# Second projection: the cast of the weight tiles moved from GpSimd to ScalarE

## The chip, the cores and the metric

The kernel runs on one core of a Trainium2 chip. The metric is the device time of one execution in microseconds (us), lower is better. All data is float32.

## The reference

Two transformer-like layers stand one behind the other, over 2048 latent tokens and 256 context tokens of width 1024. The part that matters here is the entry of the second layer: the tokens are normalised and projected by one 1024 x 2816 weight, and the first 1024 output channels feed a gated depthwise convolution of 31 taps over the tokens.

```python
def dwconv(x, w, b):            # w: 31 taps x 512 channels
    y = lax.conv_general_dilated(x, w[:, None, :], (1,), [(K // 2, K // 2)], ...)
    return y + b

def conformer_conv(a_val, a_gate, conv_w, conv_b, ln_g, ln_b):
    u = a_val * sigmoid(a_gate)
    u = dwconv(u, conv_w, conv_b)
    ...                         # layer norm, silu
```

The other 1792 channels are queries, keys, values and gates for attention and the output projection.

## The kernel before, in words

`program` (line 2892) runs the stages one after the other, each in its own scope that ends with a barrier of all engines. The stage of this document is `norm_project` (line 162), called for the second layer as `p2` with `conv` given (line 2929). The same function serves the other two layers without `conv`; the lines that differ are chosen by `if conv`.

The first half of the function normalises the tokens and leaves them transposed in SBUF as `hT`, split in a high part (fp32r) and a low part (the rest), 8 slices of 128 channels by 2304 tokens. The second half, from line 419, multiplies by the weight. It is cut in M = 22 tiles of 128 output channels. A tile `n` is a 128 x 1024 piece of weight, double-buffered (`w_sb[n % 2]`), and it is also split: `split_high` (line 144) casts it to fp32r, `split_low` (line 149) subtracts that from the original. Each product is three matmuls (high x high, high x low, low x high, lines 157 to 159).

The engines run own queues, in this order:

- SyncE (lines 442 to 459) loads the weight of tile `n` once the split of tile `n-2` is done. At tiles 4, 6, 8, 9, 11, 13 and 14 it also stores the finished convolution group `i-2` (`keep_taps`) and loads the inputs of the next one (`load_group`), which were written by the projection itself. `load_group(i)` waits for the stores of the projection tiles that it reads, for the taps of group `i-2` and for the gating of group `i-1`.
- GpSimd (lines 463 to 471) makes cast and low part of each tile `n` from 1 on. It waits for the load, and until TensorE has finished tile `n-2`, whose buffer it is.
- TensorE (lines 475 to 483) waits for the split of tile `n` and then does its chunks of tokens: four of 512 and one of 256, 24 matmuls each, every chunk in its own PSUM bank.
- ScalarE (lines 540 to 550) copies each chunk out of PSUM, with a sigmoid for the gate tiles, and issues the store of the chunk before it. `k` counts the chunks, `n, c = divmod(k, 5)`.
- VectorE (lines 495 to 527) does the convolution alone: eight groups, each of 128 channels by half of the tokens. Even groups have 2 runs of 512 tokens, odd ones a third of 256 for the context. A group is gated (line 508), gets its first tap by a tensor_scalar for each run (line 517) and the other 30 taps by one scalar_tensor_tensor for each run and tap, both inputs in SBUF (line 520); each waits for the tap before it on the same run. Line 508 is a tensor_tensor.

The first eight tiles are ordered so that gate and value of the same channels are neighbours, so that the convolution can start when two tiles are stored. Weight tile 0 is split already in the first half of the function (line 326).

`w_high` counts the casts and `w_split` the low parts.

Of the kernel before, what the change touches and what calls it, by code (L numbers as in the profile page):

```python
# [143 lines left out]
def split_high(eng, high, x):  # L144

    return eng.tensor_copy(high, x)  # L146


def split_low(eng, low, x, high):

    return eng.tensor_tensor(low, x, high.bitcast(F32), ALU.subtract)  # L151
# [10 lines left out]
def norm_project(nc, name, x_lat, x_ctx, mod, gain, w, out, groups, ident, eps, later=(), conv=None):  # L162
# [9 lines left out]
    with ExitStack() as ctx:  # L172
# [7 lines left out]
        def weight_tiles():  # L180
            tiles = [s.sb(f"w{u}", [P, KT, P]) for u in range(2)]
            parts = [[s.sb(f"w{u}_{part}", [P, KT, P], F32R) for part in ("high", "low")] for u in range(2)]
            return tiles, parts, s.sems("w_full", 2), s.sem("w_high"), s.sem("w_split")

        weights = None if later else weight_tiles()
        with ExitStack() as ctx1:
# [31 lines left out]
            with nc.Block() as block:  # L218
                @block.sync
                def _(sp):  # L220
                    def load_x(t):
                        src, n, _, _ = TILES[t]
                        if t >= NX:
                            sp.wait_ge(xn_full, t - NX + 1)
                        sp.dma_start(x[t % NX][:], src[n * P:(n + 1) * P, :]).then_inc(x_full[t % NX], 16)
# [22 lines left out]
                    for l, (c, c_ctx, _, _, _) in enumerate(later):  # L248
                        sp.dma_start(cond[:, l, 0, :], c[0].rearrange("(p k) -> p k", k=KT)).then_inc(cond_in, 16)
                        sp.dma_start(cond[:, l, 1, :], c_ctx.rearrange("(p k) -> p k", k=KT)).then_inc(cond_in, 16)  # L250
# [133 lines left out]
        w_sb, w_part, w_full, w_high, w_split = weights or weight_tiles()  # L384
# [5 lines left out]
        b_full, b_free = s.sems("b_full", 5), s.sems("b_free", 5)  # L390
        M = len(COLS)
        CTX_BEFORE = [sum(with_ctx for _, with_ctx in COLS[:n]) for n in range(M + 1)]

        def chunks(n):
            return list(enumerate(CHUNKS if COLS[n][1] else CHUNKS[:-1]))

        def uses(n, c):

            return CTX_BEFORE[n] if c == 4 else n
# [19 lines left out]
        with nc.Block() as block:  # L419
# [41 lines left out]
            @block.gpsimd  # L461
            def _(pool):
                for n in range(0 if later else 1, M):
                    pool.wait_ge(w_full[n % 2], (n // 2 + 1) * 16)
                    if n >= 2:
                        c = 4 if COLS[n - 2][1] else 3
                        pool.wait_ge(b_full[c], uses(n - 1, c))
                    pool.sem_inc(w_part_turn, 1)
                    split_high(nc.gpsimd, w_part[n % 2][0][:], w_sb[n % 2][:]).then_inc(w_high, 1)
                    pool.wait_ge(w_high, n + 1)  # L470
                    split_low(nc.gpsimd, w_part[n % 2][1][:], w_sb[n % 2][:], w_part[n % 2][0][:]).then_inc(w_split, 1)

# [12 lines left out]
            def copy_out(eng, copy, n, mine):  # L485
                if n >= 2:
                    eng.wait_ge(o_out[n % 2], n // 2 * 16)
                for c, (t0, cnt) in chunks(n):
                    if c in mine:
                        eng.wait_ge(b_full[c], uses(n, c) + 1)  # L490
                        copy(o[n % 2][:, t0:t0 + cnt], ps[c][:, 0:cnt]).then_inc(b_free[c], 1)  # L491
# [40 lines left out]
            @block.scalar  # L532
            def _(act):
                def store_chunk(k):
                    n, c = divmod(k, 5)
                    t0, cnt = CHUNKS[c]
                    act.wait_ge(b_free[c], n + 1)
                    act.dma_start(out[COLS[n][0] * P:(COLS[n][0] + 1) * P, t0:t0 + cnt], o[k % NO][:, 0:cnt]).then_inc(o_out[k % NO], 16)

                for k in range(5 * M if conv else 0):  # L540
                    n, c = divmod(k, 5)
                    cnt = CHUNKS[c][1]
                    if k >= NO:
                        act.wait_ge(o_out[k % NO], 16 * (k // NO))
                    act.wait_ge(b_full[c], n + 1)
                    nc.scalar.activation(o[k % NO][:, 0:cnt], ps[c][:, 0:cnt], ACT.Sigmoid if n < 8 and n % 2 == 0 else ACT.Copy).then_inc(b_free[c], 1)
                    if k:
                        store_chunk(k - 1)
                if conv:
                    store_chunk(5 * M - 1)  # L550
                for n in range(0 if conv else M):
                    copy_out(act, nc.scalar.copy, n, (1, 3))
                    for c, _ in chunks(n):
                        act.wait_ge(b_free[c], uses(n, c) + 1)
                    m, width = COLS[n][0], T if COLS[n][1] else SEQ
                    act.dma_start(out[m * P:(m + 1) * P, 0:width], o[n % 2][:, 0:width]).then_inc(o_out[n % 2], 16)
                for u in range(NO):
                    act.wait_ge(o_out[u], 16 * len(range(u, 5 * M if conv else M, NO)))
# [2490 lines left out]
```

## Time and profile before

| | us |
|---|---|
| median of 3 runs | 7279.33 (7265.52 to 7285.22) |
| the profiled execution | 7282.06, its span 7280.4 |
| TensorE busy, of the span | 5664.7 (78%) |
| VectorE busy | 3688.1 (51%) |
| GpSimd busy | 2075.9 (29%) |
| ScalarE busy | 1714.0 (24%) |

The profile is one execution. Times are us from the start of the span. PE is TensorE's matmuls, PEld its weight loads, DVE is VectorE, ACT ScalarE, POOL GpSimd, SP SyncE; a letter q behind an engine is its queue. A row of a timeline gives the start, the duration, the engine, the line of the source, the operation, what is written and read, and how many instructions were merged; in square brackets stands how long the engine had idled and what released it. An instruction that is held up after its start shows as a long one. Lines 146, 151 and 157 to 159 are helpers, so their rows hold several callers; the names of the tiles tell them apart (`p_w` is the weight tile, `p_cy` the convolution's sum).

### The profile page before, as it was taken

The page shows a single profiled execution, that of the slowest core. Times are in us where ns is not written, and L with a number is a line of the kernel's source. Part 1 is how long each engine was busy: PE and PEld are TensorE (multiplying, and loading weights), DVE is VectorE, ACT ScalarE, POOL GpSimd, SP SyncE. Part 2 cuts the span into 40 slices and gives each one's busy share as a digit, 9 for nine tenths or more (in the row PEclk, how much of TensorE's full clock was granted, in tenths as well). Part 3 has the DMA queues.
Part 4 walks back from the last instruction along what each step waited for, and adds up shares of the span by engine and source line. Part 5 has one row for each costly group of instructions (what it writes and reads, how often), then busy time and mean ns, then how long its engine had stood idle before and what let it go on. Part 6 is the DMA issues. An engine that isn't in the chain of part 4 may idle for free. (4 is left out here: it accounts for less than half of the span.)

```text
span 7280.4 us, 117918 instructions
## 1 busy us (share of the span) xinstructions
PE 5664.7 (78%) x49713; PEld 4331.2 (59%) x49713; DVE 3688.1 (51%) x5261; ACT 1714.0 (24%) x3014; POOL 2075.9 (29%) x1372
## 2 busy tenths in 40 slices
PE   6899971139999556749586854999986999779989
PEld 1588850028888445627475732555574887357767
DVE  2100026654444666748499235888855000256667
ACT  2100002123332322213310021444413000124442
POOL 2211100024453312203467300766734111000002
PEclk8899985569999778879698986999996999879899
DMA  6312113332111111036322122000063211121115
GB/s 206 103 66 73 68 65 119 115 101 65 56 56 47 51 45 51 10 132 206 94 95 77 65 107 72 17 18 16 15 204 105 75 66 68 62 67 26 26 57 176
DMA packets 395963, 572.21 MB, mean 79 GB/s; under 512 B 62982, under 2 KB 296070, under 8 KB 375806
## 3 DMA queue, kind: packets, MB, share of 16 engines
q1 hardware_dynamic: 351126, 394.12, 17.4%
q10 hardware_dynamic: 33576, 127.83, 4.4%
q0 software_dynamic: 10752, 42.89, 2.1%
q8 instruction: 390, 6.39, 0.4%
q14 instruction: 119, 0.97, 0.0%
HBM read 360.86 MB, written 203.90 MB: 78 GB/s over the span
## 5 line engine op out<-in xcount | busy, mean ns | idle before, releaser
L157 PE MATMUL p_bank<-p_hT_high,p_w_high 128*128 128x512 f32 (+1 forms) x2928 | 1105.3, 377 | 139.4 <-POOL p_w_low L151 121.5
L158 PE MATMUL p_bank<-p_hT_low,p_w_high 128*128 128x512 f32 (+1 forms) x2928 | 1103.7, 377 | 0.0
L159 PE MATMUL p_bank<-p_hT_high,p_w_low 128*128 128x512 f32 (+1 forms) x2928 | 1102.7, 377 | 0.0
L491 DVE COPY p_o<-p_bank 128x512 f32<-128x512 f32 (+1 forms) x142 | 90.7, 639 | 1256.5 <-PE p_bank L159 1256.5
L146 POOL CAST p_w_high<-p_w 128x1024 fp32r<-128x1024 f32 x79 | 334.4, 4233 | 1345.7 <-issue 1152.6
L157 PEld LDWEIGHTS p_bank<-p_hT_high,p_w_high 128*128 128x128 f32 x2928 | 555.9, 190 | 242.1 <-POOL p_w_low L151 122.8
L158 PEld LDWEIGHTS p_bank<-p_hT_low,p_w_high 128*128 128x128 f32 x2928 | 555.7, 190 | 99.9
L159 PEld LDWEIGHTS p_bank<-p_hT_high,p_w_low 128*128 128x128 f32 x2928 | 555.1, 190 | 100.3
L2334 POOL TENSOR_TENSOR at_acc<-at_acc,at_p 128x512 f32<-128x512 f32 x256 | 426.4, 1665 | 142.2 <-ACT at_p L2272 120.5
L2376 DVE TENSOR_REDUCE at_mx<-at_mb 128x2 f32<-128x1024 f32 (+1 forms) x292 | 356.9, 1222 | 107.7 <-PE at_mb L2175 105.9
L1197 PE MATMUL rsc_db<-rsc_W,rsc_TK 64*64 64x64 f32 x8640 | 382.6, 219 | 4.6 <-issue 3.8
L2272 ACT ACTIVATE at_p<-at_sc 128x1024 f32<-128x1024 f32 (+1 forms) x296 | 284.9, 1013 | 400.3 <-PE at_sc L2164 348.4
L520 DVE SCALAR_TENSOR_TENSOR p_cy<-p_cu,p_wt,p_cy 128x512 f32<-128x512 f32 (+1 forms) x600 | 372.5, 700 | 0.0
L491 ACT COPY p_o<-p_bank 128x512 f32<-128x512 f32 x114 | 67.0, 588 | 1281.2 <-PE p_bank L159 1281.2
L157 PE MATMUL o_bank<-o_w_high,o_m_high 128*128 128x512 f32 x800 | 314.6, 393 | 66.9 <-POOL o_m_low L151 66.9
L1197 PEld LDWEIGHTS rsc_db<-rsc_W,rsc_TK 64*64 64x64 f32 x8640 | 355.1, 136 | 5.6 <-issue 4.5
L158 PE MATMUL o_bank<-o_w_low,o_m_high 128*128 128x512 f32 x800 | 313.4, 392 | 0.0
L159 PE MATMUL o_bank<-o_w_high,o_m_low 128*128 128x512 f32 x800 | 313.2, 391 | 0.0
L1169 POOL TENSOR_TENSOR rsc_TK<-rsc_TK,rsc_lv 128x768 f32<-128x768 f32 x108 | 195.8, 1813 | 329.4 <-DVE rsc_TK L1343 329.4
L2196 PE MATMUL at_ob<-at_p,at_V 128*64 128x512 f32 (+1 forms) x1184 | 283.3, 599 | 0.7 <-ACT at_osb L2279 0.7
L1575 DVE TENSOR_TENSOR hg_P<-hg_sc,hg_mk 128x1024 f32<-128x1024 f32 x192 | 225.8, 1218 | 110.7 <-PE hg_sc L1648 110.3
L1352 DVE TENSOR_TENSOR rsc_W<-rsc_W,rsc_db 128x512 f32<-128x512 f32 x270 | 171.1, 634 | 207.5 <-PE rsc_db L1197 205.8
(375 smaller groups left out, 11285.8 us busy)
## 6 DMA issues: line engine op xcount, KB each, us to landing
rsc_X<-rwkv_chunks SPq DMA_DIRECT2D x108, 320.0 KB, 4.5
pT<-p_o ACTq DMA_DIRECT2D x28, 1152.0 KB, 4.2
pT<-p_o ACTq DMA_DIRECT2D x29, 1024.0 KB, 3.9
o_z<-pT SPq DMA_DIRECT2D x50, 512.0 KB, 5.3
o_y<-y SPq DMA_DIRECT2D x50, 512.0 KB, 6.7
pT<-p_o ACTq DMA_DIRECT2D x88, 256.0 KB, 2.0
p_w<-in_w_in_dram SPq DMA_DIRECT2D x33, 512.0 KB, 3.9
x<-o_o ACTq DMA_DIRECT2D x32, 512.0 KB
```

Of the source, the lines that this page charges most:

```text
L146: return eng.tensor_copy(high, x)
L157: nc.tensor.matmul(out, lhs[0], rhs[0], start=start, stop=False)
L158: nc.tensor.matmul(out, lhs[0], rhs[1], start=False, stop=False)
L159: return nc.tensor.matmul(out, lhs[1], rhs[0], start=False, stop=stop)
L520: x = nc.vector.scalar_tensor_tensor(dst, src, wt[:, t, k:k + 1], dst, ALU.mult, ALU.add)
L1169: nc.gpsimd.tensor_tensor(tk[:, K_LB:K_LB + LV, d, :], tk[:, K_A:K_A + 1, d, :].broadcast_to([P, LV, P]), lv[:, d, :, :], ALU.mult).then_i ...
L1197: return nc.tensor.matmul(out, l, r, start=start, stop=stop)
L1575: nc.vector.tensor_tensor(PR[n % 2][h][:], sc[h][:], mk[:, d], ALU.mult).then_inc(sc_evac[h], 1)
L2196: m = nc.tensor.matmul(ob[h * HD:(h + 1) * HD, 0:n], V[:, tiles[j], kv * HD:(kv + 1) * HD], pr[t % 4][:, h, 0:n], start=(j == 0), stop=(t ...
L2272: nc.scalar.activation(pr[t % 4][:, :, 0:n], sc[t % 2][:, :, 0:n], ACT.Exp, scale=SC).then_inc(exp_done, 1)
L2334: nc.gpsimd.tensor_tensor(acc[b % 2][:, 1, 0:n], acc[b % 2][:, 1, 0:n], pr[t % 4][:, 1, 0:n], ALU.add).then_inc(sum_b, 1)
L2376: r = nc.vector.reduce_max(mx[b % 2][:, :, t:t + nt, c], mb[:, :, 0:nt * n].rearrange("p h (j k) -> p h j k", j=nt), AX)
```

## The change

In the stage with `conv`, GpSimd no longer casts the weight tile; the low part stays there and waits for the cast as before. ScalarE makes the cast instead: for tile 1 ahead of its first copy, and for tile `n+1` between its copies of chunk 0 and chunk 1 of tile `n`. Ahead of the cast it waits for the load of the weight tile and for the end of tile `n-1` on TensorE. GpSimd keeps its own waits. The two other calls of the function, without `conv`, are as before.

```diff
--- before.py
+++ after.py
@@ -466,7 +466,8 @@
                         c = 4 if COLS[n - 2][1] else 3
                         pool.wait_ge(b_full[c], uses(n - 1, c))
                     pool.sem_inc(w_part_turn, 1)
-                    split_high(nc.gpsimd, w_part[n % 2][0][:], w_sb[n % 2][:]).then_inc(w_high, 1)
+                    if not conv:
+                        split_high(nc.gpsimd, w_part[n % 2][0][:], w_sb[n % 2][:]).then_inc(w_high, 1)
                     pool.wait_ge(w_high, n + 1)
                     split_low(nc.gpsimd, w_part[n % 2][1][:], w_sb[n % 2][:], w_part[n % 2][0][:]).then_inc(w_split, 1)
 
@@ -537,9 +538,19 @@
                     act.wait_ge(b_free[c], n + 1)
                     act.dma_start(out[COLS[n][0] * P:(COLS[n][0] + 1) * P, t0:t0 + cnt], o[k % NO][:, 0:cnt]).then_inc(o_out[k % NO], 16)
 
+                def cast_weights(n):
+                    act.wait_ge(w_full[n % 2], (n // 2 + 1) * 16)
+                    if n >= 2:
+                        act.wait_ge(b_full[4], n - 1)
+                    nc.scalar.copy(w_part[n % 2][0][:], w_sb[n % 2][:]).then_inc(w_high, 1)
+
+                if conv:
+                    cast_weights(1)
                 for k in range(5 * M if conv else 0):
                     n, c = divmod(k, 5)
                     cnt = CHUNKS[c][1]
+                    if c == 1 and 2 <= n + 1 < M:
+                        cast_weights(n + 1)
                     if k >= NO:
                         act.wait_ge(o_out[k % NO], 16 * (k // NO))
                     act.wait_ge(b_full[c], n + 1)
```

## Rows read from the trace of the kernel before

**Rows 1.** Costliest groups of the page: line, engine, operation, count | busy us, mean ns
```profile
L146 POOL CAST p_w_high<-p_w 128x1024 fp32r<-128x1024 f32 x79 | 334.4, 4233 | 1345.7 <-issue 1152.6
```

**Rows 2.** Line 546: count, ns min/median/max, first and last start in us
```profile
L546 ACT ACTIVATE p_o<-p_bank x110: 383/597/602, 3582.4 to 4234.3; 128x512 f32<-128x512 f32 x88, 128x256 f32<-128x256 f32 x22
L546 ACT ACT_TABLE_LOAD  x1: 1283/1283/1283, 3574.8 to 3574.8; - x1
```

**Rows 3.** Groups of the stage, 3540 to 4260 us
```profile
L146 POOL CAST p_w_high<-p_w 128x1024 fp32r<-128x1024 f32 x22 | 275.3, 12514 | 282.7 <-PE p_bank L159 141.2 <-issue 140.6 <-POOLq L37 0.9
...
L151 POOL TENSOR_TENSOR p_w_low<-p_w,p_w_high 128x1024 fp32r<-128x1024 f32 x22 | 58.9, 2675 | 1.8
```

**Rows 4.** Waits of the stage: us in total, times, longest
```profile
PE p_bank L157 <- POOL p_w_low L151: 103.2, 5, 28.9
```

**Rows 5.** Timeline of GpSimd in the stage: start us, us, engine line
```profile
3651.02 30.60 POOL L146 CAST p_w_high<-p_w 128x1024 fp32r<-128x1024 f32 x1 [21.15 <-issue]
...
3684.86 1.23 POOL L146 CAST p_w_high<-p_w 128x1024 fp32r<-128x1024 f32 x1
...
3796.82 50.01 POOL L146 CAST p_w_high<-p_w 128x1024 fp32r<-128x1024 f32 x1 [4.22 <-issue]
3846.90 3.21 POOL L151 TENSOR_TENSOR p_w_low<-p_w,p_w_high 128x1024 fp32r<-128x1024 f32 x1
```

**Rows 6.** Timeline of VectorE in the stage
```profile
3638.62 1.24 DVE L508 TENSOR_TENSOR p_cu<-p_cu,p_cg 128x1039 f32<-128x1039 f32 x1 [44.72 <-DMA p_cg<-pT]
...
3640.89 39.83 DVE L520 SCALAR_TENSOR_TENSOR p_cy<-p_cu,p_wt,p_cy 128x512 f32<-128x512 f32 x60
...
3689.14 51.70 DVE L520 SCALAR_TENSOR_TENSOR p_cy<-p_cu,p_wt,p_cy 128x512 f32<-128x512 f32 x90
...
3792.98 1.32 DVE L517 TENSOR_SCALAR p_cy<-p_cu,p_wt,p_cb 128x512 f32<-128x512 f32 x3
3794.22 51.71 DVE L520 SCALAR_TENSOR_TENSOR p_cy<-p_cu,p_wt,p_cy 128x512 f32<-128x512 f32 x90
```

**Rows 7.** Timeline of ScalarE in the stage
```profile
3650.96 0.39 ACT L546 ACTIVATE p_o<-p_bank 128x256 f32<-128x256 f32 x1 [2.28 <-PE p_bank L159]
...
3656.43 0.60 ACT L546 ACTIVATE p_o<-p_bank 128x512 f32<-128x512 f32 x1 [5.08 <-PE p_bank L159]
...
3675.61 0.38 ACT L546 ACTIVATE p_o<-p_bank 128x256 f32<-128x256 f32 x1 [2.27 <-PE p_bank L159]
...
3692.18 0.60 ACT L546 ACTIVATE p_o<-p_bank 128x512 f32<-128x512 f32 x1 [16.18 <-PE p_bank L159]
...
3858.37 0.60 ACT L546 ACTIVATE p_o<-p_bank 128x512 f32<-128x512 f32 x1 [36.57 <-PE p_bank L159]
```

**Rows 8.** Stretch after a stall: busy us of engines, TensorE's clock, DMA share, GB/s
```profile
3850.00:3853.00 3.00, 2.83 (x7) 2.25 (x8) 3.00 (x3) 0.00 (x0) 2.92 (x3) 0.50 0.41 110
```

**Rows 9.** Line 637, casts in the output projection: ns min/median/max
```profile
L637 ACT CAST o_w_high<-o_w x24: 1044/1046/1057, 3279.1 to 7099.3; 128x1024 fp32r<-128x1024 f32 x24
```

**Rows 10.** GpSimd and VectorE timelines in the HGRN stage; line 1468's durations
```profile
2403.97 3.46 POOL L1468 TENSOR_TENSOR hg_lv<-hg_cum 128x512 f32<-128x512 f32 x1
...
2403.80 2.62 DVE L1550 TENSOR_TENSOR hg_ke<-hg_ke,hg_k 128x2304 f32<-128x2304 f32 x1 [6.13 <-ACT hg_ke L1504]
2406.34 3.23 DVE L1554 TENSOR_TENSOR hg_qe<-hg_qe,hg_q 128x2048 f32<-128x2048 f32 x1
...
L1468 POOL TENSOR_TENSOR hg_lv<-hg_cum x84: 1032/1097/3458, 2397.8 to 3038.5; 128x512 f32<-128x512 f32 x84
```

**Rows 11.** GpSimd and VectorE timelines in the first output projection
```profile
3280.28 2.01 POOL L146 CAST o_m_high<-o_m 128x1024 fp32r<-128x1024 f32 x1 [161.78 <-DVE o_m L695]
...
3280.17 7.62 DVE L151 TENSOR_TENSOR o_w_low<-o_w,o_w_high 128x1024 fp32r<-128x1024 f32 x4
```

**Rows 12.** SyncE's timeline, and DMA issues from 3740 to 3760: KB each, us to landing
```profile
3633.53 0.34 SPq L432 DMA_DIRECT2D p_cu<-pT  x1
...
p_cg<-pT SPq DMA_DIRECT2D x1, 519.5 KB, 5.7
```

## The prediction, made before the changed kernel was run

> **Reading order.** I read the costliest groups first, then the stage of the second projection (from 3574.8 to 4234.3 us of the span [rows 2]), its waits, and last the timelines of GpSimd, VectorE and ScalarE side by side, because a sum over the kernel hides who holds whom.
>
> **What bounds the kernel now.** The reader is to see in [rows 1] that a GpSimd cast of a 128x1024 weight tile has a mean of 4233 ns, and that within this stage the mean is 12.5 us, while the subtraction behind it (the low part) has 2.7 us [rows 3]. TensorE has nothing else to wait for: five times it idles until the low part is there, 103.2 us together [rows 4]. A tile of TensorE's work takes 24.65 us (the last-chunk copies at 3650.96 and 3675.61 [rows 7]), so 22 of them are 542 us of the 660 us of the stage; the rest is the five stalls, a slow start and the slow clock after each stall. After a stall of 28.9 us the clock is granted at 0.50, 1.2 GHz in place of 2.4 [rows 8]; the copy of the first chunk then starts at 3858.37, 8.3 us after the low part was ready (3846.90 + 3.21 [rows 5, 7]), against 5.47 us at full clock (3650.96 to 3656.43). So a long stall costs 2.8 us beyond its length; after the stall of 9 us it was 1.8 (3684.9, where the low part ends and the next cast begins, to 3692.18 [rows 5, 7]).
>
> **Who holds the cast.** The convolution is eight groups on VectorE, G0 to G7, even ones of 60 scalar_tensor_tensor (39.8 us) and odd ones of 90 (51.7 us) with no gap inside [rows 6]. The cast asked for at 3651.02 ends at 3681.62; G0's stream ends at 3680.72. The one asked for at 3796.82 ends at 3846.83; G3's stream ends at 3845.93 [rows 5, 6]. Each is held to the end of the stream and then takes its usual 1.04 us, 0.90 of it behind the stream. Not one of eight such casts, one for each group, got in between two instructions of a stream. At five of the boundaries two tiles pass now: cast and low of the held tile, then cast (3684.86) and low of the next, the last of them just ahead of the next stream at 3689.14 [rows 5, 6].
>
> **Removed.** 21 GpSimd casts, 1.04 us each when not held.
>
> **Added.** 21 ScalarE casts of 128x1024 float32 to fp32r; the same operation takes 1046 ns in the output projection [rows 9]. ScalarE's copies here take 0.60 us with 4.8 us of waiting between them [rows 7], so one cast between two copies delays nothing. Table loads: the line of the copies has one, although they alternate between Sigmoid and Copy [rows 2], so I add none. Below zero this term can't go; above, it is 21 x 1.05 = 22 us only if every one of them stood in front of TensorE; I take 0.
>
> **Moved, and this decides.** Two things. First, the cast of tile n+1 no longer starts when tile n-1 is finished, which is when TensorE starts tile n; it stands in ScalarE's queue behind the copy of tile n's chunk 0. From TensorE's start of tile n that is 5.5 + 0.6 + 1.05 + 0.1 = 7.2 us at full clock, 8.3 + 0.6 + 1.05 + 0.1 = 10.0 us after a stall, before the low part can ask. Of itself this is hidden: 24.7 + 2.8 - 10.0 - 2.4 leaves 15 us. Queued behind ScalarE's new waits are its copies and stores; the weight tile has landed long before while the queues run as below. Second, the low part stays on GpSimd and now meets the stream in the cast's place. No row shows a low part that asked during a stream. The bounds are 2.4 us (not held) and the rest of a stream, up to 50 us (held as the cast is). The nearest rows: a GpSimd tensor_tensor asked at 2403.97 beside a VectorE tensor_tensor that ends at 2406.42, and ended at 2407.43, 3.46 us where its minimum is 1.03 [rows 10]; so this form is held too, and the end is again one GpSimd duration behind VectorE's. A GpSimd cast beside VectorE tensor_tensors got in after the first of four (2.01 us) [rows 11]. Cast and tensor_tensor are thus treated alike by a VectorE tensor_tensor; what never lets go is the stream of scalar_tensor_tensor. I take: the low part is held to the end of the stream.
>
> The Trainium skill (SBUF — State Buffer, section "Who interferes with whom") says that a VectorE instruction with two SBUF inputs contends with a GpSimd instruction that reads SBUF, and that the first to issue keeps the pair for its whole instruction. The low part reads two SBUF tiles, so the rule speaks against leaving it there. Taken word for word, though, the loser waits one instruction, and 50.01 us of waiting is 70 and more of them; by the word the low part would get in after at most 0.7 us, and the time would be rival B's.
>
> **The sum, tile by tile.** Times in us of the span; S is the end of a low part, stream ends plus 2.3. Tiles 0 to 3 are as before. G0 ends 3680.7, S4 = 3683.0 (now 3684.9). TensorE had finished tile 3 at 3675.6: stall 7.5. G1: gate 1.5, tensor_scalars 1.3 [rows 6], stream from 3685.7 to 3737.4. Tile 5's low part asks at 3692, seven us too late for the boundary, where now it passes. S5 = 3739.7, tile 4 ended 3709.7: stall 30.1. G2 streams 3741.8 to 3781.6, S6 = 3783.9, stall 16.7. G3's load now is late: SyncE issues it behind the load of tile 8, which waits for S6. A load of an even group took 5.1 us from first issue to VectorE's start (3633.53 [rows 12] to 3638.62 [rows 6]); behind a weight load and a store, with landings of 5.7 us [rows 12], I take 7 us from S for an even group and 10 for an odd one (four transfers behind three). So G3 has its data at 3793.9 and would stream from 3796.7; tile 7's low part asks at 3794 and gets in. From here on:
> - G3 streams to 3850.7; S8 = 3853.0, tile 7 ended 3836: stall 17.
> - G4 to 3895.0; S9 = 3897.4, stall 17. G5 late, low 10 gets in; G5 to 3964.2.
> - S11 = 3966.5, stall 17. G6 late, data after 7 us, stream from 3975.7; low 12 asks at 3976.5, 0.8 too late. G6 to 4015.5, S12 = 4017.8, stall 24.
> - G7 late, low 13 gets in; G7 streams 4033 to 4084.7, S14 = 4087.0, stall 17.
> - Tiles 14 to 21: 8 x 24.65 + 2.6 = 199.8, end 4287.
>
> Stalls: 7.5 + 30.1 + 16.7 + 17 + 17 + 17 + 24 + 17 = 146 in place of 103, eight slow starts of 1.8 to 2.8 in place of five: +43 + 8, and 2 of rounding. The stage ends 53 us later than 4234.3. Behind it nothing overlaps it (a barrier), so all of it is paid. The profiled execution took 7282.06 (span 7280.4), 2.7 above the median of 7279.33: 7282.06 + 53 = 7335, or 7332 by the median.
>
> **Rivals.** A is the forecast. Its own spread: if low 12 gets in, G7's load is early and the end is 4277 (+43). If low 7 misses too (it has some 0.8 to 2.8 us), each such miss makes the next group's load late as well; followed through, the end is 4303 (+68). A alone, with 4 us either way: 7318 to 7351, by the median.
> B, the other side: the low part is not held, or for one instruction only. For it: [rows 10, 11] show GpSimd getting in between two back-to-back VectorE tensor_tensors. Against it: the stream never let the cast in. It decides from whether the wait stays under the 15 us of slack. Then the five stalls go, 103, and their slow starts, 12. What is late next is SyncE: the load of tile 15 stands behind G7's load, which waits for G5's end and G6's gate. TensorE would end tile 14 at 3601.6 + 14 x 24.65 = 3947. Without any holding, the six streams to G5's end take 3 x 39.8 + 3 x 51.7 = 274.5 from 3640.9, with five boundaries of 2.6: 3928, so low 15 is there just in time. If each of twelve low parts takes the port from VectorE for 2.4, G5 ends at 3957 and low 15 comes at 3967: 20 us and a slow start back. 115 - 22 = 93: 7186; at best 7165.
> C, in between: the low part is held but gets in more often than I count, once more in G1 or G2, where the stalls are longest. S5 at the first boundary would save 28 us, a second such tile some 17: 7285 to 7305.
> That the change does not do what it says: the cast ordering is explicit by a count of 1 per tile, so I give it nothing of its own.
>
> **Chances.** A 0.78, B 0.17, C 0.05. The range must leave out no more than 0.2: it leaves out B, reaches through C to 7285 and above A to 7360, for a load slower than I took. What this kernel's measurement can tell from no change is about 0.3%, 22 us: faster 0.18, same 0.05, slower 0.77.
>
> **What would show it.** Right: low parts of 16 to 50 us in the GpSimd timeline that end 2.3 us behind a stream, one tile per boundary, eight stalls of TensorE, ScalarE casts of 1.05 us. VectorE idle before G3, G5, G6 and G7. Wrong: low parts of 2.4 to 3.3 us within a stream and no stalls (B); or fewer than eight stalls (C). If the casts on ScalarE took much over 1.05 us, or a table load stood at each, the term taken as 0 is wrong.

## The result and the profile after

The changed kernel takes 7322.87 us (median of 4, 7318.9 to 7329.54) against 7279.68 us: a ratio of 1.0063, 95% interval 1.0046 to 1.0081, so 33 to 59 us slower. The forecast was 7332, the range 7285 to 7360.

The busy times of the page, for the whole kernel. ScalarE's rises by the casts (1714.0 to 1732.4). TensorE, which has the same matmuls, is busy 15.5 us longer; 8.0 of that is in this stage (556.19 to 564.15 us), where the mean granted clock is 0.89 in place of 0.91, and the rest in stages whose code did not change.

```profile
PE 5680.2 (78%) x49713; PEld 4338.1 (59%) x49713; DVE 3671.1 (50%) x5261; ACT 1732.4 (24%) x3035; POOL 2053.6 (28%) x1351
```

The line of ScalarE's copies (557 now, 546 before), and ScalarE's first instruction of the stage. The stage runs from 3566.8 to 4269.2 us, 702.4 us; before it was 3574.8 to 4234.3, 659.5 us [rows 2]. It is 42.9 us longer, which is the difference of the medians (43.2). The profiled executions differ by 39.9 (7321.91 against 7282.06); the other 3 us are stages whose code did not change: the stage begins 8.0 earlier, and what follows it takes 5.0 longer. To compare a time of this stage with one of before, add 8.0.

```profile
L557 ACT ACTIVATE p_o<-p_bank x110: 383/597/602, 3575.3 to 4269.2; 128x512 f32<-128x512 f32 x88, 128x256 f32<-128x256 f32 x22
```

```profile
3566.80 1.04 ACT L545 CAST p_w_high<-p_w 128x1024 fp32r<-128x1024 f32 x1 [4.63 <-PEq L37]
```

The waits of the stage: us in total, times, longest. Eight stalls of TensorE, 138.1 us, in place of five with 103.2 [rows 4]. VectorE waits for data four times: before G0 (44.4 us), and before G3, G5 and G6 (12.2, 11.8 and 10.4 us).

```profile
PE p_bank L157 <- POOL p_w_low L151: 138.1, 8, 30.1
DVE p_cu L509 <- DMA p_cg<-pT: 78.8, 4, 44.4
```

The groups of the stage: count | busy us, mean ns | idle before. The low part has a mean of 14.7 us (2.7 before [rows 3]); it has taken over the wait that the cast had. The cast on ScalarE takes 1.04 us.

```profile
L521 DVE SCALAR_TENSOR_TENSOR p_cy<-p_cu,p_wt,p_cy 128x512 f32<-128x512 f32 x480 | 328.1, 742 | 0.0
L151 POOL TENSOR_TENSOR p_w_low<-p_w,p_w_high 128x1024 fp32r<-128x1024 f32 x21 | 308.3, 14680 | 355.1 <-ACT p_w_high L545 355.1
...
L545 ACT CAST p_w_high<-p_w 128x1024 fp32r<-128x1024 f32 x21 | 21.9, 1042 | 4.6 <-PEq L37 4.6
```

GpSimd's timeline, the low parts of tiles 4, 5, 6, 7, 11, 12, 13 and 14:

```profile
3650.99 24.78 POOL L151 TENSOR_TENSOR p_w_low<-p_w,p_w_high 128x1024 fp32r<-128x1024 f32 x1 [22.27 <-ACT p_w_high L545]
3686.12 46.34 POOL L151 TENSOR_TENSOR p_w_low<-p_w,p_w_high 128x1024 fp32r<-128x1024 f32 x1 [10.36 <-ACT p_w_high L545]
3741.81 34.79 POOL L151 TENSOR_TENSOR p_w_low<-p_w,p_w_high 128x1024 fp32r<-128x1024 f32 x1 [9.35 <-ACT p_w_high L545]
3786.07 2.39 POOL L151 TENSOR_TENSOR p_w_low<-p_w,p_w_high 128x1024 fp32r<-128x1024 f32 x1 [9.46 <-ACT p_w_high L545]
...
3923.66 34.13 POOL L151 TENSOR_TENSOR p_w_low<-p_w,p_w_high 128x1024 fp32r<-128x1024 f32 x1 [22.55 <-ACT p_w_high L545]
3967.15 2.40 POOL L151 TENSOR_TENSOR p_w_low<-p_w,p_w_high 128x1024 fp32r<-128x1024 f32 x1 [9.35 <-ACT p_w_high L545]
3991.81 20.43 POOL L151 TENSOR_TENSOR p_w_low<-p_w,p_w_high 128x1024 fp32r<-128x1024 f32 x1 [22.26 <-ACT p_w_high L545]
4021.38 47.54 POOL L151 TENSOR_TENSOR p_w_low<-p_w,p_w_high 128x1024 fp32r<-128x1024 f32 x1 [9.14 <-ACT p_w_high L545]
```

VectorE's timeline beside it, the streams of G0, G1 and G2, then the boundary ahead of G6 with its stream, and that of G7:

```profile
3633.73 39.84 DVE L521 SCALAR_TENSOR_TENSOR p_cy<-p_cu,p_wt,p_cy 128x512 f32<-128x512 f32 x60
...
3678.55 51.72 DVE L521 SCALAR_TENSOR_TENSOR p_cy<-p_cu,p_wt,p_cy 128x512 f32<-128x512 f32 x90
...
3734.57 39.83 DVE L521 SCALAR_TENSOR_TENSOR p_cy<-p_cu,p_wt,p_cy 128x512 f32<-128x512 f32 x60
...
3966.00 1.24 DVE L509 TENSOR_TENSOR p_cu<-p_cu,p_cg 128x1039 f32<-128x1039 f32 x1 [10.38 <-DMA p_cg<-pT]
3967.34 2.95 DVE L518 TENSOR_SCALAR p_cy<-p_cu,p_wt,p_cb 128x512 f32<-128x512 f32 x2
3970.21 39.83 DVE L521 SCALAR_TENSOR_TENSOR p_cy<-p_cu,p_wt,p_cy 128x512 f32<-128x512 f32 x60
...
4015.01 51.71 DVE L521 SCALAR_TENSOR_TENSOR p_cy<-p_cu,p_wt,p_cy 128x512 f32<-128x512 f32 x90
```

The reader is to see the ends. The low part of tile 5 ends at 3686.12 + 46.34 = 3732.46, G1's stream at 3678.55 + 51.72 = 3730.27: 2.2 us apart, which is one undisturbed low part. Tile 4's ends 2.2 behind G0's stream (3675.77 and 3673.57), tile 6's 2.2 behind G2's (3776.60 and 3774.40). Only the held tile passes at the first two of these boundaries. The low parts of tiles 7 and 12 are short, because the data of G3 and G6 came late. Tile 7's asked while VectorE still stood idle before G3. Tile 12's asked during the gating of G6 (3966.00 to 3967.24), 3 us before its stream begins (3967.15 and 3970.21), and VectorE's two tensor_scalars are the ones that wait (2.95 us).

### The profile page after: what moved, and what is told of

Its sections match the earlier page's. It is cut to its first block and busy times, and to the rows that moved or that the text cites. A ratio compares the mean times of both kernels' runs of the same rounds, so it can differ in the third digit from the quotient of the medians.

```text
span 7320.3 us, 117938 instructions
## 1 busy us (share of the span) xinstructions
PE 5680.2 (78%) x49713; PEld 4338.1 (59%) x49713; DVE 3671.1 (50%) x5261; ACT 1732.4 (24%) x3035; POOL 2053.6 (28%) x1351
## 5 line engine op out<-in xcount | busy, mean ns | idle before, releaser
L151 POOL TENSOR_TENSOR p_w_low<-p_w,p_w_high 128x1024 fp32r<-128x1024 f32 x79 | 447.1, 5660 | 359.7 <-ACT p_w_high L545 355.1
L146 POOL CAST p_w_high<-p_w 128x1024 fp32r<-128x1024 f32 x58 | 60.6, 1045 | 1063.8 <-issue 1012.0
```

## The experiments

Each kernel was profiled. Times are medians, or one run where the text says so, beside the kernel before on the same chip: 7285.1 us for e1, e2, e3 and e6, 7279.3 for e5, e7, e8 and e9, 7284.0 for e10 to e13. The stage lengths are from the line of the copies and the start of the stage, as above.

**e1_early: the same engines, asked earlier.**

```diff
-                    if c == 1 and 2 <= n + 1 < M:
+                    if c == 0 and 2 <= n + 1 < M:
                         cast_weights(n + 1)
```

> The changed kernel with one move: ScalarE makes the cast of tile n+1 ahead of its copy of chunk 0 of tile n, not behind it, so the cast is done while TensorE still waits for tile n and the next low part can ask before the stream ends. Theory 1 (an operation on GpSimd that asks during a stream of scalar_tensor_tensor is held to its end, and the loss came from the second tile asking too late for the boundary): two tiles pass at a boundary again, five stalls as in the kernel before and each about 1.9 us shorter, since the cast no longer stands in the boundary: 7265 to 7275 us. Theory 2 (only one GpSimd operation gets through a boundary, or the cast on ScalarE itself costs the time, wherever it stands): eight stalls and 7315 to 7325 us as in the changed kernel.

Measured: 7274.47 us, ratio to before 0.9983 (0.9973 to 0.9992). The waits of TensorE, and GpSimd's timeline (a row with x2 is two low parts in a row):

```profile
PE p_bank L157 <- POOL p_w_low L151: 94.7, 5, 27.0
```

```profile
3655.78 33.64 POOL L151 TENSOR_TENSOR p_w_low<-p_w,p_w_high 128x1024 fp32r<-128x1024 f32 x2 [22.27 <-ACT p_w_high L545]
3715.08 33.22 POOL L151 TENSOR_TENSOR p_w_low<-p_w,p_w_high 128x1024 fp32r<-128x1024 f32 x2 [25.66 <-ACT p_w_high L545]
```

Five stalls again, 94.7 us, and two low parts in one boundary. The stage is 649.7 us long (3578.0 to 4227.7), 9.8 less than before. So the move of the cast to ScalarE is worth a small gain by itself, about the 5 x 1.9 us expected, and the place in ScalarE's queue costs it more than five times over: 702.4 - 649.7 = 52.7 us.

**e2_pool_late: the old engine, asked later.**

```diff
                         pool.wait_ge(b_full[c], uses(n - 1, c))
+                        if conv:
+                            pool.sem_inc(w_part_turn, 1)
+                            pool.wait_ge(b_full[0], n)
```

> The kernel before with one more wait: GpSimd makes the cast as before, but begins it only when TensorE has finished chunk 0 of the tile ahead, which is about when the changed kernel makes it. Theory 1 (the late asking is what costs, on whichever engine the cast runs): one tile for each boundary, eight stalls or so, 7315 to 7340 us. Theory 2 (the move to ScalarE costs by itself): 7275 to 7290 us as the kernel before.

Measured: 7335.84 us (one run), eight stalls:

```profile
PE p_bank L157 <- POOL p_w_low L151: 144.8, 8, 31.3
```

The kernel before, with nothing changed but that GpSimd asks one chunk later, shows the whole loss and some us more (the stage is 708.1 us long), since the cast again stands in each boundary. With e1_early this says that the moment of asking makes the loss, not the engine.

**e3_tt: another instruction in the stream.** It leaves out the multiplication by the tap's weight.

```diff
-                                x = nc.vector.scalar_tensor_tensor(dst, src, wt[:, t, k:k + 1], dst, ALU.mult, ALU.add)
+                                x = nc.vector.tensor_tensor(dst, src, dst, ALU.add)
```

> The changed kernel with the 30 later taps of each run done by a tensor_tensor add in place of the scalar_tensor_tensor: same shapes, same two SBUF inputs, same waits; it leaves out the multiplication by the tap's weight. Theory 1a (the scalar_tensor_tensor itself never lets GpSimd in): now the low parts get in after at most one or two instructions, 2.4 to 5 us each, no or nearly no stalls, 7165 to 7195 us. Theory 1b (any back-to-back stream with two SBUF inputs and such waits holds): low parts of 16 to 50 us, eight stalls, 7310 to 7330 us.

Measured: 7279.46 us (one run). Theory 1a fell. GpSimd's and VectorE's timelines:

```profile
3688.96 41.38 POOL L151 TENSOR_TENSOR p_w_low<-p_w,p_w_high 128x1024 fp32r<-128x1024 f32 x1 [9.86 <-ACT p_w_high L545]
```

```profile
3681.88 46.27 DVE L521 TENSOR_TENSOR p_cy<-p_cu,p_cy 128x512 f32<-128x512 f32 x90
```

A stream of 90 tensor_tensors holds the low part to its end just as well (3730.34, 2.2 us behind 3728.15). Theory 1b holds by its low parts, but not by its figures: it expected eight stalls and 7310 to 7330 us, and there are seven, 102.5 us. These instructions are quicker, 46.27 us in place of 51.72 for a stream, so each held wait is shorter.

**e10_swap, e11_out: the operands.** e10 exchanges the two inputs of e3_tt's add; e11 writes its output to a tile of its own, which also leaves out the summing of the taps.

```diff
-                                x = nc.vector.tensor_tensor(dst, src, dst, ALU.add)
+                                x = nc.vector.tensor_tensor(dst, dst, src, ALU.add)                  # e10_swap
+                                x = nc.vector.tensor_tensor(cz[:, at:at + n], src, dst, ALU.add)     # e11_out
```

> Experiment e3_tt (a tensor_tensor add for each later tap, the multiplication by the tap's weight left out) with its two inputs exchanged: the sum is now the first input and the shifted signal the second. In the HGRN stage the tile that is also the output stands first, and there GpSimd got in between two instructions. Theory O (the order of the inputs, or which of them is the output, decides): low parts of 2.4 to 5 us and 7170 to 7200 us. Theory N (it does not): as e3_tt, 7270 to 7290 us, low parts of 16 to 43 us.

> Experiment e3_tt with the output of the add in a tile of its own, so that the instruction no longer writes one of its inputs; the summing of taps is thereby left out as well as their weights. Theory A (writing one's own input is what keeps GpSimd out): low parts of 2.4 to 5 us, 7170 to 7200 us. Theory N: as e3_tt, 7270 to 7290 us.

Measured: 7291.52 and 7287.87 us (one run each), the first 1.5 us above the figure of its theory N. Low parts up to 43.75 us and 42.88 us, seven stalls each. One of e11_out:

```profile
3690.58 41.39 POOL L151 TENSOR_TENSOR p_w_low<-p_w,p_w_high 128x1024 fp32r<-128x1024 f32 x1 [9.87 <-ACT p_w_high L546]
```

Neither the order of the inputs nor the writing of one's own input decides.

**e7_two_acc, e12_one_wait: the waits.** Both keep two accumulators and leave out their sum. In e7 each instruction waits for the tap two before it, four or six instructions back; in e12 only the first run of a tap has a wait at all.

```diff
-                            src, dst = u[:, base + k:base + k + n], y[:, at:at + n]
-                            if k == 0:
+                            src, dst = u[:, base + k:base + k + n], (y, cz)[k % 2][:, at:at + n]
+                            if k <= 1:
...
-                                dve.wait_ge(tap_done, TAPS[i] + (k - 1) * len(RUNS[half]) + r + 1)
+                                dve.wait_ge(tap_done, TAPS[i] + (k - 2) * len(RUNS[half]) + r + 1)   # e7_two_acc
+                                if r == 0:                                                           # e12_one_wait
+                                    dve.wait_ge(tap_done, TAPS[i] + (k - 1) * len(RUNS[half]))
```

> The changed kernel with two accumulators: even taps are summed in the old tile and odd ones in a second one, so each tap waits for the tap two before it, four or six instructions back in place of two or three. It leaves out the sum of the two. Theory F (the port stays taken because each instruction's wait ends just as its forerunner of two back ends, with the next one right behind): with waits that have long been met GpSimd gets in after an instruction or two as in the HGRN stage, low parts of 2.4 to 5 us, 7170 to 7200 us. Theory S (any unbroken stream of such instructions on VectorE, whatever its waits): low parts held to the end of a stream, 7315 to 7325 us.

> Experiment e7_two_acc (two accumulators, the final sum left out) with one wait for each tap, at its first run, in place of one for each instruction, so the second and third run of a tap follow with no wait of their own, as the instructions in the HGRN stage do. Theory W2 (an instruction that carries a wait leaves no opening before it, one without a wait does): low parts of 2.4 to 5 us, 7170 to 7200 us. Theory N (waits have nothing to do with it): as e7_two_acc, 7305 to 7325 us.

Measured: 7312.99 and 7328.11 us (one run each), eight stalls in both, 135.3 and 135.9 us, low parts up to 48.70 us in both. The time of the second is 3 us above the figure of theory N. Neither earlier waits nor fewer of them open the stream. A stream with no wait at all was not tried.

```profile
PE p_bank L157 <- POOL p_w_low L151: 135.9, 8, 31.3
```

**e5_gap: something small between the instructions.**

```diff
...
                     for k in range(K):
+                        nc.vector.memset(gap[:, i * K + k:i * K + k + 1], 0.0).then_inc(gap_done, 1)
                         for r, (at, n, base) in enumerate(RUNS[half]):
```

> The changed kernel with a memset of one column of a scratch tile on VectorE ahead of each tap, so after every two or three instructions of a stream there is one that has no SBUF input. Experiment e3_tt showed that the held wait does not hang on the scalar_tensor_tensor. Theory S (GpSimd is only kept out while one two-input instruction follows another without a break): low parts of 2.4 to 5 us, no stalls, 7170 to 7200 us. Theory W (it is the way in which the stream's instructions wait for each other that keeps it out, and a memset between them changes nothing): low parts of 16 to 50 us, 7315 to 7340 us.

Measured: 7187.31 us (one run), 92 us under the kernel before in the same round and 136 us under the changed kernel. GpSimd's timeline, VectorE's around the first of these low parts, and the waits of TensorE and ScalarE:

```profile
3654.30 2.54 POOL L151 TENSOR_TENSOR p_w_low<-p_w,p_w_high 128x1024 fp32r<-128x1024 f32 x1 [22.27 <-ACT p_w_high L547]
3678.96 2.73 POOL L151 TENSOR_TENSOR p_w_low<-p_w,p_w_high 128x1024 fp32r<-128x1024 f32 x1 [22.12 <-ACT p_w_high L547]
```

```profile
3652.50 1.42 DVE L523 SCALAR_TENSOR_TENSOR p_cy<-p_cu,p_wt,p_cy 128x512 f32<-128x512 f32 x2
3653.20 0.06 DVE L516 MEMSET p_gap<- 128x1 f32 x1
3653.84 3.55 DVE L523 SCALAR_TENSOR_TENSOR p_cy<-p_cu,p_wt,p_cy 128x512 f32<-128x512 f32 x2
3654.54 0.06 DVE L516 MEMSET p_gap<- 128x1 f32 x1
3657.31 1.41 DVE L523 SCALAR_TENSOR_TENSOR p_cy<-p_cu,p_wt,p_cy 128x512 f32<-128x512 f32 x2
```

```profile
ACT p_w_high L547 <- DMA p_w<-in_ab_w_in_dram: 43.8, 3, 35.5
...
PE p_bank L157 <- POOL p_w_low L151: 20.7, 1, 20.7
```

A memset of 0.06 us is the opening. The low part asks at 3654.30 and takes 2.54 us; it is VectorE that waits now, 3.55 us for two instructions that take 1.42. Undisturbed, two instructions and the memset take 1.34 us (3652.50 to 3653.84), and two instructions without it took 39.83 / 30 = 1.33 [rows 6]. One stall is left, of 20.7 us: ScalarE wants to cast tile 15 and its weight has not landed.

**e8_chain: every instruction waits for the one just before it.**

```diff
-                    for k in range(K):
-                        for r, (at, n, base) in enumerate(RUNS[half]):
+                    for r, (at, n, base) in enumerate(RUNS[half]):
+                        for k in range(K):
...
-                                dve.wait_ge(tap_done, TAPS[i] + (k - 1) * len(RUNS[half]) + r + 1)
+                                dve.wait_ge(tap_done, TAPS[i] + r * K + k)
```

> The changed kernel with the two loops of the convolution exchanged: all 31 taps of a run, then the next run. Each tap now waits for the instruction just before it, so VectorE drains after every one. Same work. Theory S (GpSimd is kept out by the overlap of one instruction with the next): it gets in at the first end of an instruction, low parts of 2.4 to 4 us, no stalls, VectorE's convolution longer by some 0.1 us for each of 600 taps and 2.3 us for each low part, still ended before TensorE: 7170 to 7200 us. Rival (held by the stream as such): low parts of 16 to 55 us, 7325 us and more.

Measured: 7248.25 us, ratio 0.9953 (0.9936 to 0.9971). GpSimd gets in, low parts of 2.4 to 2.9 us, but the time was missed by 50 us:

```profile
ACT p_w_high L545 <- DMA p_w<-in_ab_w_in_dram: 128.5, 4, 57.7
...
PE p_bank L157 <- POOL p_w_low L151: 69.1, 4, 42.7
```

```profile
3848.56 23.59 DVE L521 SCALAR_TENSOR_TENSOR p_cy<-p_cu,p_wt,p_cy 128x512 f32<-128x512 f32 x30
```

A 128x512 instruction no longer overlaps its neighbour. Thirty of them with no low part among them take 23.59 us, 0.79 us each, where the changed kernel had 39.83 / 60 = 0.66. That is the 0.1 us that was expected. What the expectation had wrong is that this would stay hidden. The convolution becomes so long that SyncE, which waits for its groups, loads four weight tiles late: four stalls, 69.1 us. They are put down to the low part, but that waited for the cast, and the cast for the load, 57.7 us at worst.

**e6_dve_low, e9_sp, e13_gap_sp: the stage without the stalls.** e6 takes the low part away from GpSimd; VectorE does it at fixed taps, and the cast is early as in e1. e9 is e6 with SyncE's group loads one tile later in its queue. e13 is e5 with that queue and e1's early cast.

```diff
+                def low(n):
+                    dve.wait_ge(w_high, n + 1)
+                    split_low(nc.vector, w_part[n % 2][1][:], w_sb[n % 2][:], w_part[n % 2][0][:]).then_inc(w_split, 1)
...
                     for k in range(K):
+                        if k in LOW_AT[i]:          # {18: 4} in G0, {4 or 6: 2i + 3, 20: 2i + 4} in the others
+                            low(LOW_AT[i][k])
...
-            GROUPS_AT = {4: (0, 1), 6: (2,), 8: (3,), 9: (4,), 11: (5,), 13: (6,), 14: (7,)}
+            GROUPS_AT = {5: (0, 1), 7: (2,), 9: (3,), 10: (4,), 12: (5,), 14: (6,), 15: (7,)}    # e9_sp, e13_gap_sp
```

> The changed kernel with GpSimd taken out of the split altogether: the cast on ScalarE ahead of chunk 0, and the low part on VectorE, tiles 1 to 3 ahead of the convolution, two of the tiles 4 to 18 at fixed taps within each group (one in the first), 19 to 21 behind it. Theory 1 (all stalls of this stage come from GpSimd being held): no stall above some 5 us, VectorE's stream some 20 us longer and still ended long before TensorE, the stage near 22 x 24.65 + 10 us: 7165 to 7180 us, faster than both kernels. Rival (the gain is given back, since VectorE's queue stands waiting for casts or SyncE's queue loads a weight late behind a group): some stalls of 10 us and more come back, 7190 to 7250 us.

> Experiment e6_dve_low (no GpSimd in the split) with SyncE's queue changed: the stores and loads of the convolution groups stand behind the load of the next weight tile, one tile later than before. In e6_dve_low one stall of 6.5 us was left, at tile 15, whose weight SyncE loaded behind the last group's inputs. Theory 1 (that stall is SyncE's order): no stall is left, some 9 us less than e6_dve_low in the same round: 7165 to 7180 us. Rival (a group's inputs now come too late and VectorE idles, which delays a low part): 7185 to 7200 us.

> Experiment e5_gap (a memset of one column on VectorE ahead of each tap, low part on GpSimd, cast on ScalarE) with the cast ahead of chunk 0 and with SyncE's queue as in e9_sp. In e5_gap one stall of 20.7 us was left, at tile 15, whose weight tile landed late behind the last group's inputs. Theory 1 (that stall is SyncE's order alone): no stalls, 20 to 25 us less than e5_gap: 7155 to 7175 us, level with e9_sp. Rival (with VectorE's stream some 45 us longer the late loads of the groups move the stall elsewhere): 7180 us and more.

Measured: e6 7183.55 us, 4 us above its expectation, ratio 0.9851 (0.9826 to 0.9876); e9 7166.86 us, 0.9838 (0.9819 to 0.9857); e13 7168.54 us, 0.9841 (0.9824 to 0.9857). The waits of TensorE for the low part in e6 and in e9, and in e13 its one wait of the stage that has a name:

```profile
PE p_bank L157 <- DVE p_w_low L151: 6.5, 1, 6.5
```

```profile
PE p_bank L157 <- DVE p_w_low L151: 1.7, 2, 1.4
```

```profile
PE p_bank L157 <- PEq L37: 8.9, 1, 8.9
```

e6 has one stall, 6.5 us, at tile 15; with SyncE's queue changed 1.7 us are left, and in e13 none at all (8.9 us is the start of the stage, which all these kernels have). The three intervals overlap, so the order among them is shown by the traces and not by the times. e9 differs from e6 only in SyncE's queue, so that stall is SyncE's order. e13 differs from e5 in SyncE's queue and in the early cast, and does not separate the two. All three are about 100 to 115 us faster than the kernel before, which is what the stage had to give in stalls and slow starts, and 139 to 156 us faster than the changed kernel.

## Why the prediction was right, point by point

**The held low part: right, and the heart of it.** No low part that asked during a stream was in the trace of before. The forecast took it from casts that were held, and the trace after shows held low parts in all eight streams, each ending 2.2 us behind one (2.3 was taken).

**The late asking: right.** A tile asks 9.4 us after the end of the low part before it when TensorE comes out of a stall (3957.79, the end of the row at 3923.66, to 3967.15); 10.0 was taken. The rows of ScalarE show why it is less: the copy starts 7.7 us after the low part's end and not 8.3, and the cast 0.5 us after the copy's start and not behind its end.

```profile
3965.53 0.60 ACT L557 ACTIVATE p_o<-p_bank 128x512 f32<-128x512 f32 x1 [24.19 <-PE p_bank L159]
3966.03 1.04 ACT L545 CAST p_w_high<-p_w 128x1024 fp32r<-128x1024 f32 x1
```

e1_early and e2_pool_late show from two sides that this is the term that decides.

**The sum, by its own steps.** With 8.0 added, the ends of the low parts are: S4 3683.8 (3683.0 forecast), S5 3740.5 (3739.7), S6 3784.6 (3783.9), S8 3853.1 (3853.0), S9 3897.3 (3897.4), S11 3965.8 (3966.5). All six lie within 0.8 us. Within them one term was off: tile 4's slow start cost 3.3 us (its first copy at 3684.51, 8.7 us after the low part's end at 3675.77, against 5.47), where the sum had 2.

**The step that was off: tile 12.** The forecast let it miss G6's boundary by 0.8 us, and had a stall of 24 us there and one of 17 us at tile 14. Both terms of that race were mis-sized: G6's data came 8.2 us behind S11 (3966.00) and not 7, and the low part asked at 9.4 and not 10.0. So it got in, and VectorE did not stand idle before G7. G6's stream caught tile 13 instead, with a stall of about 3 us (from ScalarE's copy of tile 12's last chunk at 4009.38 to the low part's end at 4012.24), and G7's stream, begun earlier, held tile 14's low part for a stall of 30 us. The count of eight stalls was right by chance: tile 13 stands in the place of tile 12. The text had this branch, with an end at 4277; measured, 4269.2 + 8.0 = 4277.2. The 53 us forecast became 43.

**What was taken as 0.** The casts on ScalarE took 1.04 us each, and there is one table load, as before. Right.

**The rivals.** B did not happen in this kernel, but e5_gap made it happen: with GpSimd let in, low parts of 2.4 to 2.9 us, VectorE delayed by each, and SyncE's queue late for tile 15. Its price was given as 7186 with a stall of 20 us; measured, 7187.31 (one run) and 20.7. The weight that B was given rested on GpSimd getting in between two tensor_tensors elsewhere [rows 10, 11]. C did not happen.

**What the text blamed and should not have.** It said that the stream of scalar_tensor_tensor never lets go, as against tensor_tensor. e3_tt refutes that: in the same place tensor_tensors hold as well.

**The rule.** The Trainium skill (SBUF — State Buffer, section "Who interferes with whom") says that whoever issues first has the shared pair for its whole instruction while the other is blocked. Word for word, the loser waits for one instruction. That the two contend agrees with the trace: the low part of 47.54 us ends 2.2 us behind G7's stream. How long it waits does not: some 45 us, near 80 instructions. The measurement decides: in an unbroken stream of this kind the loser waits for the end of the stream.

**What stays open.** Why VectorE's tensor_tensors in the HGRN stage and in the output projection let GpSimd in after one [rows 10, 11] and those of the convolution do not. It is not the operation (e3_tt), the order of inputs (e10_swap), the tile written (e11_out), the age of the waits (e7_two_acc) or a wait on every instruction (e12_one_wait). Nor is it the counting up of a semaphore by each instruction: the four in the output projection do that too, and so do the two tensor_tensors of a gating, between which the kernel before let a low part in.

```profile
3788.33 2.02 DVE L508 TENSOR_TENSOR p_cu<-p_cu,p_cg 128x1039 f32<-128x1039 f32 x1
3789.33 3.26 POOL L151 TENSOR_TENSOR p_w_low<-p_w,p_w_high 128x1024 fp32r<-128x1024 f32 x1
3790.27 2.61 DVE L508 TENSOR_TENSOR p_cu<-p_cu,p_cg 128x256 f32<-128x256 f32 x1
```

The low part asks at 3789.33 during the first, waits for its end, and the second is then the one held: 2.61 us where the changed kernel shows 0.41 for it when undisturbed. In all these places the instruction before the opening has 1024 elements or more for each partition, in the streams 512 or 256. The sizes and the shifted input were not tried.

## What to carry to other kernels

When an operation is held by another engine's stream, moving it away only hands the hold to the next operation of the chain on the same engine; look at what follows it. If a boundary between streams is the only opening, the time at which an operation asks is worth more than its duration: here asking one chunk later, 5.5 to 8.3 us, cost 53 us. Better than catching the openings is to make one: with a memset of 0.06 us every few instructions the changed kernel went from 7322.87 to 7187.31 us (one run), 92 us under the kernel before, and then the next queue (SyncE's) had to be looked after.

## What the runs showed of the hardware that I had not expected

- VectorE instructions with two SBUF inputs, back to back, kept GpSimd out to the end of the stream, whether scalar_tensor_tensor or tensor_tensor. The longest low part was 47.54 us (after), 42.83 (e3_tt), 43.75 (e10_swap), 42.88 (e11_out) and 48.70 (e7_two_acc and e12_one_wait), of which some 2.4 are its own.
- One memset of a single column between them, 59 ns, lets GpSimd in at once: the wait falls to at most 0.6 us (low parts of 2.39 to 2.94 us in e5_gap), and it costs VectorE nothing that shows in a tap's time.
- A wait for the instruction just before lets GpSimd in too (e8_chain), at 0.79 us for each 128x512 tap in place of 0.66, since neighbours no longer overlap.
